# A Fourier stage with tokens folded before the transform and 65 channel columns per part

## The reference

```
def _fourier_group(z):
    B, S, _ = z.shape                                   # S = 1024
    zg = z.astype(jnp.float32).reshape(B, S, N_FOURIER_GROUPS, FOURIER_GROUP_DIM)   # 4 groups of 128
    y = jnp.fft.fft2(zg, axes=(1, 3), norm='ortho').real
    return y.reshape(B, S, FOURIER_WIDTH).astype(z.dtype)
```

## Time and profile before

| What | Value |
|---|---|
| Median of 3 runs | 3781.57 us (3771.51 to 3787.52) |
| The profiled execution | 3770.92 us |
| Its span in the trace | 3769.1 us, mean granted clock 0.97 |
| PE busy | 3586.4 us (95%) |
| DVE busy | 1824.0 us (48%) |
| ACT busy | 1216.4 us (32%) |
| Channel stage | about 2688 to 2716.78 us |
| Token stage | 2716.78 to 2768.46 us |
| mLSTM stage | 2768.46 to about 2890 us |

### The profile page before, as it was taken

The page is one execution under the profiler, slowest core; times in us unless marked ns, Lnnn a source line. Parts: engine busy times, 40 slices in busy tenths (PEclk is TensorE's granted clock), DMA queues, the critical chain, the costliest instruction groups (busy, mean ns, idle before and its releaser), DMA issues. The chain is left out here.

```text
span 3769.1 us, 41502 instructions
## 1 busy us (share of the span) xinstructions
PE 3586.4 (95%) x16012; PEld 2865.7 (76%) x16012; DVE 1824.0 (48%) x2293; ACT 1216.4 (32%) x1746; POOL 519.0 (14%) x287
## 2 busy tenths in 40 slices
PE   8979999999998999879999999999977899999998
PEld 6757888888786777648888888888766678888886
DVE  7986423232266666655322233555357874323235
ACT  4335411111244444454311112444432353212123
POOL 0016100000061000035000000451001540000004
PEclk9989999999999999989999999999977999999999
DMA  2102213122132111102222132232221223111113
GB/s 100 36 31 79 95 61 100 50 89 72 47 102 59 40 45 50 45 17 90 84 76 85 44 117 90 93 96 95 69 73 40 78 73 95 56 45 50 45 56 101
DMA packets 75999, 261.17 MB, mean 69 GB/s; under 512 B 10224, under 2 KB 10608, under 8 KB 75888
## 3 DMA queue, kind: packets, MB, share of 16 engines
q1 hardware_dynamic: 75888, 259.69, 21.6%
HBM read 246.54 MB, written 4.72 MB: 67 GB/s over the span
## 5 line engine op out<-in xcount | busy, mean ns | idle before, releaser
L197 PE MATMUL ps<-xh,whi 128*128 128x512 f32 x2816 | 982.4, 394 | 45.6 <-DVE wlo L180 19.0
L197 PE MATMUL ps<-xl,whi 128*128 128x512 f32 x2816 | 974.5, 391 | 0.0
L197 PE MATMUL ps<-xh,wlo 128*128 128x512 f32 x2816 | 974.3, 391 | 0.0
L180 DVE TENSOR_TENSOR wlo<-stage,whi 128x1024 fp32r<-128x1024 f32 x366 | 524.9, 1434 | 514.6 <-ACT whi L174 513.5
L174 ACT ACTIVATE whi<-stage 128x1024 fp32r<-128x1024 f32 x366 | 386.5, 1056 | 1080.4 <-PE ps L197 1032.7
L197 PEld LDWEIGHTS ps<-xh,whi 128*128 128x128 f32 x2816 | 532.3, 189 | 164.6 <-issue 30.6
L197 PEld LDWEIGHTS ps<-xh,wlo 128*128 128x128 f32 x2816 | 532.0, 189 | 111.4
L197 PEld LDWEIGHTS ps<-xl,whi 128*128 128x128 f32 x2816 | 532.5, 189 | 109.8
L197 PE MATMUL ps<-hh,whi 128*128 128x512 f32 x1216 | 422.6, 396 | 6.0 <-ACT lam_t L2050 3.9
L197 PE MATMUL ps<-hl,whi 128*128 128x512 f32 x1216 | 421.5, 395 | 0.0
L197 PE MATMUL ps<-hh,wlo 128*128 128x512 f32 x1216 | 421.5, 395 | 0.0
(11 more groups left out here) (371 smaller groups left out, 3906.0 us busy)
## 6 DMA issues: line engine op xcount, KB each, us to landing
stage<-in_w_ff SPq DMA_DIRECT2D x88, 512.0 KB, 3.6
stage<-in_w_gate SPq DMA_DIRECT2D x59, 512.0 KB, 3.3
stage<-in_w_up SPq DMA_DIRECT2D x59, 512.0 KB, 3.3
stage<-in_w_in SPq DMA_DIRECT2D x50, 512.0 KB, 3.2
ada<-in_w_ada SPq DMA_DIRECT2D x48, 512.0 KB, 3.4
stage<-in_w_qkv SPq DMA_DIRECT2D x43, 512.0 KB, 3.4
stage<-in_w_down SPq DMA_DIRECT2D x48, 448.0 KB, 3.4
stage<-in_w_out SPq DMA_DIRECT2D x32, 512.0 KB, 3.2
```

The lines of the kernel that those rows point to most:

```text
L180: dve.tensor_tensor(wlo[slot][:], stage[slot][:], whi[slot][:].bitcast(F32), ALU.subtract).then_inc(w_split, 1)
L197: done = pe.matmul(acc[:, h * HALF:(h + 1) * HALF], wt[slot][:, w], xt[:, b, h * HALF:(h + 1) * HALF], start=b == 0 and wt is whi and xt i ...
```

## The change

Each Fourier block of `zt` is folded by DVE behind the splits of units 12 to 15 of `in2b` (`fold`). The sum and the difference of tokens n and n + 512 replace them; the sums are folded once more at distance 256. The outputs at k = 4j then need 256 folded tokens (2 token blocks), those at 4j + 2 another 256, and the odd ones 512. The token matrix shrinks from 8 units to 3: unit 0 holds cosine and sine for t = 0 and t = 1, units 1 and 2 those for t = 2 and t = 3. Of each part of the channel transform only columns 0 to 64 are formed, since the rest are their mirror images: a channel matmul has 130 columns, a token matmul 4 x 65 = 260. The mirrored channels are written by DVE, which now adds and subtracts in 4 instructions for each t. `yf` is written with token steps of 4 or 2. The alternating sums read 256 tokens in place of 1024. As `dft` has 5 units fewer, every later unit changes its slot.

```
-    plan["dft"] = Product(NT, blocks(io["dft"]))
+    plan["dft"] = Product(3, blocks(io["dft"]))
...
+    Z_AT = 9
+    folded = arena[:, 16 * S:16 * S + HALF]
+    def fold(dve, b):
+        z, quarter = zt[:, b, :], HALF // 2
+        dve.wait_ge(acc_free, i2b.base + Z_AT + b + 3)
+        if b:
+            dve.wait_ge(z_fold, 4 * b)
+        else:
+            dve.wait_ge(gs, 8)
+        dve.tensor_tensor(folded, z[:, 0:HALF], z[:, HALF:S], ALU.add).then_inc(z_fold, 1)
+        dve.tensor_tensor(z[:, HALF:S], z[:, 0:HALF], z[:, HALF:S], ALU.subtract).then_inc(z_fold, 1)
+        dve.wait_ge(z_fold, 4 * b + 2)
+        dve.tensor_tensor(z[:, 0:quarter], folded[:, 0:quarter], folded[:, quarter:HALF], ALU.add).then_inc(z_fold, 1)
+        dve.tensor_tensor(z[:, quarter:HALF], folded[:, 0:quarter], folded[:, quarter:HALF], ALU.subtract).then_inc(z_fold, 1)
...
                 gates_dve(dve, u)
+                if u >= Z_AT + 2 and u - Z_AT - 2 < 4:
+                    fold(dve, u - Z_AT - 2)
...
-                    done = pe.matmul(ps[n % 2][:, g * 2 * P:(g + 1) * 2 * P], zt[:, g, n * P:(n + 1) * P], cs, start=True, stop=True)
+                    at = (g // 2) * HALF + (g % 2) * 2 * PART
+                    done = pe.matmul(ps[n % 2][:, at:at + 2 * PART], zt[:, g, n * P:(n + 1) * P], cs, start=True, stop=True)
...
             for t in range(NT // 2):
-                pe.wait_ge(acc_free, gdft.base + 2 * t)
+                u = dft_unit(t)
+                slot, kbs = (gdft.base + u) % 2, 2 if t < 2 else 4
+                pe.wait_ge(w_split, gdft.base + u + 3)
+                if t >= 2:
+                    pe.wait_ge(y_out, Y0 + 4 * (t - 1))
+                else:
+                    pe.wait_ge(acc_free, gdft.base + 2)
                 for k in range(2):
-                    slot = (gdft.base + k) % 2
-                    pe.wait_ge(w_split, gdft.base + 2 * t + k + 3)
-                    for b in range(DB):
+                    for b in range(kbs):
+                        w = ((t * 4 if t < 2 else 0) + k * kbs + b) * P
+                        n = (2 * t if t < 2 else 4) + b
                         for wt, xt in ((whi, xhv), (whi, xlv), (wlo, xhv)):
-                            done = pe.matmul(ps[t % 2][:, k * HALF:(k + 1) * HALF], wt[slot][:, b * P:(b + 1) * P], xt[:, NT * k + b, :],
-                                             start=b == 0 and wt is whi and xt is xhv, stop=b == DB - 1 and wt is wlo)
+                            done = pe.matmul(ps[t % 2][:, k * HALF:k * HALF + WIDE], wt[slot][:, w:w + P], xt[:, n, k, :],
+                                             start=b == 0 and wt is whi and xt is xhv, stop=b == kbs - 1 and wt is wlo)
...
+            split_hi(act, gdft, 0, 1)
             for t in range(NT // 2):
...
+                act.activation(y_sin[t % 2][:, 0:WIDE], ps[t % 2][:, HALF:HALF + WIDE], ACT.Copy).then_inc(q_out, 1)
+                if t == 1:
+                    split_hi(act, gdft, 0, 2)
                 if t:
                     out_of(t - 1)
...
-                dve.tensor_tensor(y_sum[t % 2], ps[t % 2][:, 0:HALF], y_sin[t % 2], ALU.add).then_inc(y_out, 1)
-                dve.tensor_tensor(y_dif[t % 2], ps[t % 2][:, 0:HALF], y_sin[t % 2], ALU.subtract).then_inc(y_out, 1)
...
+                for dst, straight, turned in ((y_sum, ALU.add, ALU.subtract), (y_dif, ALU.subtract, ALU.add)):
+                    to = grouped(dst[t % 2])
+                    dve.tensor_tensor(to[:, :, 0:PART], a, b, straight).then_inc(y_out, 1)
+                    dve.tensor_tensor(to[:, :, back], a[:, :, inner], b[:, :, inner], turned).then_inc(y_out, 1)
```

More of the change, by code:

```diff
@@ L2241, in program @@
     ones_col = sem("ones_col")
-    cs_in, ch_mm, ch_hi, ch_lo, q_out, y_out, y_tr, yf_out = [sem(n) for n in (
-        "cs_in", "ch_mm", "ch_hi", "ch_lo", "q_out", "y_out", "y_tr", "yf_out")]
+    cs_in, ch_mm, ch_hi, ch_lo, q_out, y_tr, yf_out = [sem(n) for n in (
+        "cs_in", "ch_mm", "ch_hi", "ch_lo", "q_out", "y_tr", "yf_out")]
     ch_alt, row_tr, row_out, dec_mm, kv_tr, kv_out = [sem(n) for n in ("ch_alt", "row_tr", "row_out", "dec_mm", "kv_tr", "kv_out")]
-    cs = arena[:, 16 * S:16 * S + 2 * P]
-    alt = [arena[:, 16 * S + 2 * P + 4 * n:16 * S + 2 * P + 4 * n + 4] for n in range(3)]
+    PART = P // 2 + 1
+    WIDE = 4 * PART
+    cs = arena[:, 16 * S:16 * S + 2 * PART]
+    cos_all = arena[:, 16 * S + 2 * PART:16 * S + 2 * PART + P]
+    CS = 2 * PART + P
+    alt = [arena[:, 16 * S + CS + 4 * n:16 * S + CS + 4 * n + 4] for n in range(3)]
     def half_tiles(n):
@@ L2252, in program @@
     y_sin, y_sum, y_dif = half_tiles(10), half_tiles(11), half_tiles(16)
-    xhv, xlv = [t[:].rearrange("p a (b n) -> p (a b) n", n=HALF) for t in (xh, xl)]
+    xhv, xlv = [t[:].rearrange("p a n -> p (a n)")[:, 0:2 * NT * WIDE].rearrange("p (b e n) -> p b e n", b=NT, e=2) for t in (xh, xl)]
     colt = sb("colt", [P, 3, NT, 2, MH], at=mix_scope)
@@ L2256, in program, with by_bank, transformed @@
     KV = 6
+    def by_bank(t):
+        return t.rearrange("p (b g c) -> p b g c", b=2, g=2)
+    def transformed(n, e):
+        return ps[n % 2][:].rearrange("p (b m) -> p b m", b=2)[:, :, 0:4 * PART].rearrange("p b (g m) -> p b g m", g=2)[:, :, :, e * PART:(e + 1) * PART]
     with nc.Block(no_gpsimd_drain=True) as block:
@@ L2300, in _ @@
             pe.wait_ge(kv_out, KV - 1)
-            pe.matmul(ps[2][:, 0:4], cs[:, 0:P], alt[2], start=True, stop=True)
+            pe.matmul(ps[2][:, 0:4], cos_all, alt[2], start=True, stop=True)
         @block.scalar
@@ L2317, in channels @@
                 act.wait_ge(ch_mm, n + 1)
-                part = ps[n % 2][:].rearrange("p (g e c) -> p g e c", g=4, e=2)
                 for e in range(2):
-                    act.activation(xhv[:, NT * e + n, :].rearrange("p (g c) -> p g c", g=4), part[:, :, e, :], ACT.Copy).then_inc(ch_hi, 1)
+                    act.activation(by_bank(xhv[:, n, e, :]), transformed(n, e), ACT.Copy).then_inc(ch_hi, 1)
             def values_keys(n):
@@ L2356, in _, with dft_unit, dft_tokens @@
                     dve.memset(v1[:, :, :, MDV:MDV + 1], 1.0).then_inc(ones_col, 1)
+    FIRST_K = (0, 2, 1, HALF // 2 + 1)
+    def dft_unit(t):
+        return max(t - 1, 0)
+    def dft_tokens(t, mirrored):
+        step, first = (4 if t < 2 else 2), FIRST_K[t]
+        if not mirrored:
+            return slice(first, first + step * P, step)
+        skip = 1 if t == 0 else 0
+        return slice(S - first - step * skip, S - first - step * P, -step)
     with nc.Block(no_gpsimd_drain=True) as block:
@@ L2410, in _, with grouped @@
         def _(dve):
+            def grouped(t):
+                return t.rearrange("p (g c) -> p g c", g=4)
+            split_lo(dve, gdft, 0, 1)
             for t in range(NT // 2):
-                split_lo(dve, gdft, t, 1)
-                if t + 1 < NT // 2:
-                    split_lo(dve, gdft, t, 2)
+                if t == 2:
+                    split_lo(dve, gdft, 0, 2)
                 dve.wait_ge(q_out, t + 1)
@@ L3142, in more_layouts, with token_part @@
     io["c_rows"] = np.ascontiguousarray(np.broadcast_to(a["c_2"].reshape(1, D), (P, D)))
-    turn = 2.0 * np.pi * (np.outer(np.arange(S), np.arange(S)) % S) / S
-    token = np.stack([unit_layout(np.cos(turn) * S ** -0.5), unit_layout(-np.sin(turn) * S ** -0.5)], axis=1)
-    io["dft"] = np.ascontiguousarray(token[:NT // 2].reshape(NT, P, S).astype(np.float32))
+    def token_part(ks, blocks):
+        turn = 2.0 * np.pi * (np.outer(np.arange(blocks * P), ks) % S) / S
+        return [f.reshape(blocks, P, P).transpose(1, 0, 2).reshape(P, blocks * P) for f in (np.cos(turn), -np.sin(turn))]
+    k = np.arange(P)
+    units = [token_part(4 * k, 2) + token_part(4 * k + 2, 2), token_part(2 * k + 1, 4), token_part(2 * (k + P) + 1, 4)]
+    io["dft"] = np.ascontiguousarray(np.stack([np.concatenate(u, axis=1) for u in units]) * S ** -0.5).astype(np.float32)
     turn = 2.0 * np.pi * (np.outer(np.arange(P), np.arange(P)) % P) / P
-    io["dft_channel"] = (np.concatenate([np.cos(turn), np.sin(turn)], axis=1) * P ** -0.5).astype(np.float32)
+    few = slice(0, P // 2 + 1)
+    io["dft_channel"] = (np.concatenate([np.cos(turn)[:, few], np.sin(turn)[:, few], np.cos(turn)], axis=1) * P ** -0.5).astype(np.float32)
 def kernel(**inputs):
```

40 lines of the change are left out of this document (23 added, 17 removed).

## The result

The changed kernel takes 3733.25 us (median of 4 runs, 3731.24 to 3740.68), the kernel before 3780.74 (4 runs). The ratio is 0.9878 with a 95% interval of 0.9856 to 0.9900: 1.2% faster, 47.5 us by the medians. The forecast was 3739.5, 42.1 us less.

The account below looks back on a forecast made before the run. TensorE (PE busy 95% of the span) was taken as the bound. The token stage's 34.4 us and the channel stage's 7.7 make 42.1 off the median 3781.57: 3739.5 us, range 3723 to 3763, chance 0.62.

Parts of the forecast that it names:

- The sum: Token stage 34.4 us less plus channel stage 7.7 less: 42.1 off the median 3781.57, giving 3739.5.
- The matmul of 260 columns: Token stage: priced by columns at 0.108 + 0.014 = 0.122 us at the high clock, 0.217 at the low.
- The rule on row groups: Skill's rule that loads overlap only across differing row groups; load plus stream would be about 0.21 us. The prediction rejected it.
- the first rival: Token stage: width brings nothing below 0.21 us a matmul, so 6.5 us more, 3746; chance 0.12.
- The second rival: Clock stays at its lower level through channel and token stages: 18.6 us more, 3758; chance 0.17.
- The fold: DVE in `in2b`: 2.1 us a block, hidden, costing nothing; 8.4 us if uncovered or late, 3748, chance 0.06.
- The channel stage: Gain 7.7 us: first two rounds 1.4, next six 5.3 (1.87 us a round), tail 1.0.
- The token stage's stall: TensorE waits 0.7 us after t = 1's matmuls, before t = 0's transposes, for ACT and four DVE pieces.
- ACT's writes: Token stage: `yf` writes with steps of 4 or 2 tokens priced like straight ones; double cost would add 1.1 us in the tail.
- The mLSTM stage: Kept at its length, 121.54 us, plus or minus 5 us for how the two clock levels fall.
- the prediction's own sign of being wrong: Prediction counts as wrong if later units stall or the mLSTM stage changes by more than 5 us.
- Slots: Rival: 104 later units change slot; if each showed DVE's 1.23 us split, 128 us slower, 3868; chance 0.03.

Follow-up runs that it names:

- number 12: The kernel before, unchanged, executed once more for its trace: channel stage 28.8 us, token stage 52.9, rest of the span 1010.8.
- number 6: The changed kernel, unedited, executed once more with a trace: 3740.45 us against 3776.25 for the kernel before, ratio 0.9894.
- Number 4: Changed kernel with each 260-column token matmul split into two of 130, each with its own weight load: 3745.34 us, ratio to the kernel before 0.9905.
- number 7: Changed kernel with each head and direction's mLSTM matmuls issued as 8 of 128 rows, then 7 of 64: 3719.85 us, ratio to the kernel before 0.9834.
- 10: The kernel before with the mLSTM matmuls regrouped by row count, Fourier stage as it was: 3762.93 us against 3780.62, ratio 0.9960.
- number 2: The kernel before with only the 65 columns (260-column token, 130-column channel matmuls), 8 units, no fold: 3750.62 us against 3779.64, ratio 0.9925.
- number 3: Changed kernel with all four folds moved behind DVE's last split of the input product: 3746.33 us against 3733.25 for the changed kernel.
- number 5: Changed kernel with yf written at neighbouring tokens for every t, output placing left out: single time 3738.95 us, token stage 16.83.
- number 8: Changed kernel with 26 and 34 unread 512-column matmuls filling TensorE's first two mLSTM waits: 3731.23 us, ratio to the kernel before 0.9871.

## Why the prediction was right

**The sum.** 43.1 us in the two stages against 42.1 in the text. Token stage 34.6 against 34.4, channel stage 8.5 against 7.7. The median came out 47.5 lower, 5.4 more than forecast; the interval of the ratio, 38 to 54 us, takes in both. A second pair of traces has 44.7 in the two stages (number 12), and a second set of runs 35.8 by the medians (number 6). So the mechanism is confirmed by the two stages, and the timing by itself couldn't tell 43 from 42.

**The matmul of 260 columns** cost 0.12 us as taken. Number 4 shows what stands near it: a floor of 0.11. The price by columns was right at this width; it reaches the floor at (0.11 - 0.014) x 2400 = 230 columns, an estimate, and below that it would have been wrong.

**The rule on row groups** would have had load and stream in series. At 260 columns that is refuted: 0.12 leaves no room for a load in series. For the pairs by turns in the mLSTM stage, 0.21 a pass, number 7 shows that they cost more just where the row counts differ. The Trainium skill, "TensorE: Matmul & The Clock Gate", "What overlaps and what doesn't", states that a weight load overlaps running matmuls only when the row group differs. These traces don't agree: the load is hidden where all matmuls have the same 128 rows, and it waits where 128 rows follow 64. My reason against the first rival, that the turn was the cause, had been an argument; numbers 7 and 10, and the loads shown with number 7, now bear it out.

**The low clock.** The second rival did not come: the granted clock was 0.92 and 0.90 over the two stages, which is some 3.3 us at the low level in each, about as foreseen. All eight traces with this token stage show 0.90 over it. Number 4 and number 2, with other matmuls there, have 0.81 and 1.00.

**The fold** took 2.0 us a block on DVE (4.21 to 2.21 idle, 2.1 foreseen) and was hidden; number 3 shows the price without cover, 5 us of waiting and 2 of clock.

**The channel stage** was under-sized by 0.8. The first rounds took 3.49 us (2694.80 to 2698.29) for 3.8, and a round 1.77 for 1.87: transposes and passes of 130 columns stand 0.11 apart and not 0.117, since I had read the step from a piece behind a wait: such a piece takes 1.09 us and one in the stream 1.04, as 2725.25 and 2715.65 above show again. The tail took 2.0 us, 0.9 less than before to the border that the prediction used, 2716.78. The first transfer, from which the stages are counted here, came 0.3 later than that border in the kernel before, so 0.3 of the 0.8 lies in the counting, and by the prediction's border the token stage gained 0.3 more.

**The token stage's stall** of 0.7 us before the first transposes did not come. The low clock fell over the end of t = 0 and most of t = 1, some 15 matmuls from 2712.1 to 2715.4, and not over the 12 of t = 0, so TensorE was late itself and the transposes had nothing to wait for. Three more slow matmuls and one stall less leave the stage at 16.9 us for 17.3; its tail, from 2723.15 to 2727.83, took the 4.7 foreseen.

**ACT's writes** with a step of 4 tokens were not like straight ones, as I had said, but twice as dear (1.09 and 1.20 to 0.60). They belong to t = 0 and t = 1 alone and were hidden (number 5). That the two in the tail have a step of 2 and cost 0.62 was luck: the prediction hadn't told the steps apart.

**The mLSTM stage.** "Plus or minus 5 us" was mis-sized. It has two lengths 6 to 7 us apart, and the whole rest of the span moves by 9 to 10. By the prediction's own sign of being wrong, a change of over 5 us here, the 141.45 us of number 6 would have told against it, though the kernel before has 141.91 too. The movement is more than the difference between forecast and result, so the last microseconds of the agreement mean nothing.

**Slots.** Later units kept their pace on changed slots; behind the mLSTM stage both kernels need 866 us in their first executions (3769.1 - 2903.13 and 3729.9 - 2863.36).

## What to carry to other kernels

Price a narrower matmul with a weight load of its own by columns only down to a floor, 0.11 us here; below that only fewer matmuls help. Matmuls with different row counts that take turns are worth sorting by row count: it gave 18 to 21 us here by the medians for a reordering, nearly half of what the whole Fourier change gave. And before a difference of some microseconds is put down to an edit, look at whether the stages that it didn't touch have the same length and granted clock in both traces.

## What the runs showed of the hardware

- TensorE, rounded-type matmuls with a weight load each, from start to start at the high clock: 0.227 us at 512 columns, 0.12 at 260, 0.11 at 130; at the low clock 0.43, 0.22 and 0.21. Passes of 8 columns are 0.11 apart too.
- A float32 pass of 129 columns is 0.12 us among passes of the same row count and 0.21 when 128 and 64 rows take turns, at the high clock; the load behind a turn doesn't run ahead of its matmul.
- TensorE's clock can fall in the middle of a stream: in number 8, between 2750.4 and 2751.5. Behind 1.9 us of idle time at the token stage's start it fell within the first matmuls in the changed kernel and in number 4 (0.90 and 0.81 over the stage), and stayed at 1.00 in number 2. In the mLSTM stage the same instructions take 135 or 142 us. What decides where it falls was not settled by these runs; that it is not the kernel's text alone is shown by numbers 6 and 12.
- ACT writing float32 to SBUF, 512 columns: 0.60 us side by side, 0.62 with a step of 2 elements, 1.09 to 1.20 with a step of 4. The Trainium skill, "SBUF — State Buffer", "Door 1: The DMA port swizzle", tells of lines of 16 bytes that need at least two hits each for full bandwidth; that fits a step of 2 elements as free and a step of 4 as dear. Its next sentence, that one can stride over 4 float32 for free, doesn't agree with the 1.09.
